# Gating tables of a product-key expert layer: GpSimd makes finished rows for two of four token groups, ScalarE scales the other two, VectorE none

## What is computed

```python
def peer(h, w_q, subkeys, u_tab, v_tab):     # 8 heads, 128 x 128 = 16384 experts, top 16
    q = (xb @ w_q).reshape(PEER_BLOCK, PEER_HEADS, PEER_QDIM)
    ...
    e = i1 * PEER_N_KEYS + i2                # 8 x 16 experts per token
    g = softmax(cs)                          # and a gate for each
    a = gelu(einsum('pd,phkd->phk', xb, u_tab[e]))
    return einsum('phk,phkd->pd', g * a, v_tab[e])
```

## Time and profile before

| | |
|---|---|
| median of 3 executions | 3304.9 us (3303.24 to 3307.88) |
| the profiled execution, its time | 3311.35 us |
| the profiled execution, its span in the trace | 3309.6 us |
| busy PE, DVE, ACT, POOL | 93%, 51%, 50%, 46% of the span |
| gating stage of layer 0 | about 695 to 805 us |
| gating stage of layer 1 | about 1815 to 1925 us |

### The profile page before, as it was taken

The page is one execution under the profiler, slowest core; times in us unless marked ns, Lnnn a source line. Parts: engine busy times, 40 slices in busy tenths (PEclk is TensorE's granted clock), DMA queues, the critical chain, the costliest instruction groups (busy, mean ns, idle before and its releaser), DMA issues.

```text
span 3309.6 us, 56035 instructions
## 1 busy us (share of the span) xinstructions
PE 3078.3 (93%) x18286; PEld 2726.7 (82%) x18286; DVE 1702.8 (51%) x2944; ACT 1666.8 (50%) x3149; POOL 1528.7 (46%) x1220
## 2 busy tenths in 40 slices
PE   8989999987999987999899699999999989999998
PEld 7679999976778866889899677877678779999997
DVE  6633370047888835173400878886301425555555
ACT  2123777788455533167677965555113224555554
POOL 3957998875444443178888644442551000000000
PEclk8979999999999997999999999999999979999999
DMA  6535554521766642345455056664664224555554
GB/s 246 195 133 181 171 171 165 182 78 57 254 228 226 231 141 89 132 140 179 157 179 176 0 184 241 234 222 139 210 208 142 91 81 154 187 186 184 184 185 132
DMA packets 153450, 552.42 MB, mean 167 GB/s; under 512 B 16896, under 2 KB 19712, under 8 KB 153232
## 3 DMA queue, kind: packets, MB, share of 16 engines
q1 hardware_dynamic: 151136, 547.42, 48.7%
q10 hardware_dynamic: 2224, 3.87, 0.4%
HBM read 550.17 MB, written 1.05 MB: 167 GB/s over the span
## 4 chain that ended last, share of the span: by engine, by line
PE 69%; ACT 9%; issue 8%; POOL 7%; DVE 4%; DMA 2%; ACTq 0%; DVEq 0%; POOLq 0%; SPq 0%; PEldq 0%
PE bank L901 19%; PE bank L875 16%; PE bank L1164 11%; PE bank L668 10%; PE bank L1182 5%; ACT hT L1352 5%; POOL w_parts L2285 4%; ACT hT L1348 2%; POOL arena L2317 1%; POOL arena L2319 1%; PE bank L687 1%; DMA ring<-stream 1%; PE bank L1146 1%; DMA arena<-stream 1%; PE bank L630 1%
## 5 line engine op out<-in xcount | busy, mean ns | idle before, releaser
L2285 POOL TENSOR_TENSOR w_parts<-ring,w_parts 128x512 fp32r<-128x512 f32 x512 | 687.2, 1368 | 193.6 <-ACT w_parts L1312 188.8
L875 PE MATMUL bank<-h_parts,w_parts 128*128 128x256 f32 x6144 | 747.5, 284 | 25.1 <-POOL w_parts L2285 23.1
L875 PEld LDWEIGHTS bank<-h_parts,w_parts 128*128 128x128 f32 x6144 | 743.2, 193 | 29.8 <-POOL w_parts L2285 26.8
L1312 ACT ACTIVATE w_parts<-ring 128x512 fp32r<-128x512 f32 x512 | 321.6, 630 | 205.6 <-PE bank L875 201.6
L668 PE MATMUL bank<-hT,ring 128*128 128x256 f32 x1584 | 361.8, 391 | 40.2 <-ACT hT L1245 32.4
L2236 DVE TENSOR_TENSOR w_parts<-ring,w_parts 128x512 fp32r<-128x512 f32 x384 | 265.3, 692 | 244.8 <-ACT w_parts L1505 236.9
L668 PEld LDWEIGHTS bank<-hT,ring 128*128 128x128 f32 x1584 | 308.4, 196 | 92.7 <-issue 33.6
L1164 PEld LDWEIGHTS bank<-h_parts,w_parts 128*128 128x128 f32 x3072 | 374.9, 193 | 5.6 <-issue 3.3
L1164 PE MATMUL bank<-h_parts,w_parts 128*128 128x256 f32 x3072 | 375.8, 284 | 2.6 <-DVE w_parts L2236 2.6
L1505 ACT ACTIVATE w_parts<-ring 128x512 fp32r<-128x512 f32 x384 | 242.2, 632 | 267.7 <-PE bank L1164 174.7
L901 PE MATMUL bank<-h_parts,a_parts 128*128 128x512 f32 x1536 | 366.2, 394 | 6.1 <-DVE a_parts L1995 6.1
(11 more groups left out here) (317 smaller groups left out, 4086.2 us busy)
## 6 DMA issues: line engine op xcount, KB each, us to landing
ring<-stream SPq DMA_DIRECT2D x786, 512.0 KB, 3.3
arena<-stream SPq DMA_DIRECT2D x192, 512.0 KB, 4.3
hT<-stream SPq DMA_DIRECT2D x32, 512.0 KB, 4.4
mean<-stream SPq DMA_DIRECT2D x32, 512.0 KB, 4.5
arena<-consts ACTq DMA_DIRECT2D x1, 1536.0 KB, 6.8
xT<-xin ACTq DMA_DIRECT2D x1, 1024.0 KB, 10.6
out<-hT SPq DMA_DIRECT2D x4, 256.0 KB, 2.2
arena<-subk ACTq DMA_DIRECT2D x2, 128.0 KB, 2.1
```

What stands on the lines that cost most here:

```text
L875: mm = pe.matmul(bank[k][:, 0:T], w[:, wp, ws], h_parts[:, hp, 4 * j + q, :], start=(j == 0 and q == 0 and i == 0), stop=(j == 1 and q == ...
L1312: act.activation(w_parts[half % HALVES][:, 0, :], ring[slot_][:, j * 512:(j + 1) * 512], ACT.Copy).then_inc(sem(f"{n}_high"), 1)
L2285: pool.tensor_tensor(w[:, 1, :], ring[(base + k) % RING][:, j * 512:(j + 1) * 512], w[:, 0, :].bitcast(F32), ALU.subtract).then_inc(sem(f" ...
```

## The change

Group 3 moves from ACT and group 1 from DVE, both to POOL. For these two groups POOL no longer subtracts but makes the finished rows, token by token, with one instruction for each of the four tokens: (row of 0..127 == index) * gate, index and gate being columns of `route`. So POOL issues two instructions of 128x512 and eight of 128x128 in a turn, where it issued four of 128x512. ACT keeps the groups 0 and 2. DVE's `picked` and its copy of the gates go. POOL's loop over the turns is written out. The semaphores follow: `diff` counts two groups a turn, and `made_hot` takes the place of `picked_hot`.

```diff
-SCALED_G = (0, 2, 3)
-PICKED_G = 1
+SCALED_G = (0, 2)
+MADE_G = (1, 3)
...
-                    if k == PICKED_G:
-                        pe.wait_ge(sem(f"{n}_picked_hot"), it + 1)
+                    if k in MADE_G:
+                        pe.wait_ge(sem(f"{n}_made_hot"), it * len(MADE_G) + (MADE_G.index(k) + 1))
...
-                    act.wait_ge(sem(f"{n}_diff"), it * GROUPS + (k + 1))
+                    act.wait_ge(sem(f"{n}_diff"), it * len(SCALED_G) + (i + 1))
...
-            iota_p, gates_p = bank[0][:, 0:P], bank[0][:, P:P + T]
-            dve.tensor_copy(iota_p, iota)
-            dve.tensor_copy(gates_p, route[:, 2, :]).then_inc(signal("dve_step"), 1)
+            iota_p = bank[0][:, 0:P]
+            dve.tensor_copy(iota_p, iota).then_inc(signal("dve_step"), 1)
...
-            def picked(it):
-
-                k = PICKED_G
-                dve.wait_ge(sem(f"{n}_diff"), it * GROUPS + (k + 1))
-                part = hot1[:, 4 * k:4 * k + 4, :]
-                dve.scalar_tensor_tensor(part, part, 0.0, gates_p[:, bass.ds(it * TURN + 4 * k, 4)].unsqueeze(2)
-                                         .broadcast_to([P, 4, P]), ALU.is_equal, ALU.mult).then_inc(sem(f"{n}_picked_hot"), 1)
...
-            with pool.Fori(0, T // TURN) as it:
+            for it in range(T // TURN):
                 for k in range(GROUPS):
+                    tokens = slice(it * TURN + 4 * k, it * TURN + 4 * k + 4)
 
                     pool.wait_ge(sem(f"{n}_hot_free"), it * GROUPS + (k + 1))
-                    pool.tensor_tensor(hot1[:, 4 * k:4 * k + 4, :], iota.unsqueeze(1).broadcast_to([P, 4, P]),
-                                       route[:, 0, bass.ds(it * TURN + 4 * k, 4)].unsqueeze(2).broadcast_to([P, 4, P]),
-                                       ALU.subtract).then_inc(sem(f"{n}_diff"), 1)
+                    if k in SCALED_G:
+                        pool.tensor_tensor(hot1[:, 4 * k:4 * k + 4, :], iota.unsqueeze(1).broadcast_to([P, 4, P]),
+                                           route[:, 0, tokens].unsqueeze(2).broadcast_to([P, 4, P]),
+                                           ALU.subtract).then_inc(sem(f"{n}_diff"), 1)
+                    else:
+                        for s, t in enumerate(range(tokens.start, tokens.stop)):
+                            ins = pool.tensor_scalar(hot1[:, 4 * k + s, :], iota, route[:, 0, t:t + 1],
+                                                     route[:, 2, t:t + 1], ALU.is_equal, ALU.mult)
+                        ins.then_inc(sem(f"{n}_made_hot"), 1)
```

More of the change, by code:

```diff
@@ L1962, in ones2 @@
                                   ALU.is_equal).then_inc(sem(f"{n}_hot2"), 1)
-            def picked(it):
-                k = PICKED_G
-                dve.wait_ge(sem(f"{n}_diff"), it * GROUPS + (k + 1))
-                part = hot1[:, 4 * k:4 * k + 4, :]
-                dve.scalar_tensor_tensor(part, part, 0.0, gates_p[:, bass.ds(it * TURN + 4 * k, 4)].unsqueeze(2)
-                                         .broadcast_to([P, 4, P]), ALU.is_equal, ALU.mult).then_inc(sem(f"{n}_picked_hot"), 1)
             for k in range(GROUPS):
                 ones2(0, k)
-                if k == PICKED_G + 1:
-                    picked(0)
             with dve.Fori(0, T // TURN - 1) as it:
@@ L1979, in peer_dve @@
                     ones2(it + 1, k)
-                    if k == PICKED_G + 1:
-                        picked(it + 1)
             for k in range(GROUPS):
```

## The result

The changed kernel takes **3354.4 us** in the median (3350.7 to 3361.9), the kernel before 3306.4 in the same comparison: ratio **1.0144**, 95% interval 1.0118 to 1.0170. I had forecast 3261.4 us in a range of 3243 to 3308. The change made the kernel 48 us slower, and it went the way of rival (d), further than its bounds reached.

What follows compares the result with a forecast made beforehand. ACT's three groups, 6.6 us a turn, were taken to bound the gating stages. POOL's turn of 2.0 + 8p would replace them, saving 145.2 - 248p, 43.5 us at p = 0.41: 3261.4 us, range 3243 to 3308.

Steps and rivals of the forecast that it cites:

- rival (d): Gating stages: POOL's queue replaces ACT's and is slower, from p = 0.585; 3317 us at p = 0.635; chance 0.14.
- What bounds the kernel: Gating stages: a turn costs three ACT groups of 2.20 us, 6.6 us; the stage is 109.9 us per layer.
- The terms for ACT, DVE and PE: Per gating turn: ACT loses 2.20 of 6.6 us, leaving 4.4; DVE falls to 4.8; PE stays at 4.1 to 4.6.
- DVE's limit of 4.8 us: Gating turn: four table products and four comparisons left on DVE, 8 x 0.60 us, the floor if POOL is cheaper.
- POOL's price p: Start-to-start time of POOL's new 128x128 instruction in the gating stages, taken as 0.41 us from the 128x128 addition.
- 145.2 - 248p: Microseconds saved over both layers' gating stages, p in us; 43.5 at 0.41, nothing left at 0.585.
- The bounds of p: POOL's new instruction: low end 0.355 us from subtraction's element cost, high end 0.706 us, the dearest 128x128 row.
- The figures of the Trainium skill: POOL's new instruction: 1.03 cycles an element gives p = 0.25; two reads of 102 cycles, 0.17 us, would make 0.58.
- What costs nothing: Gating stages: POOL's written-out loop of 160 instructions a layer, ACT's short instructions and the `hot_free` waits were given zero.
- `hot_free` waits: Before POOL's groups: already met, as group 2 is free after some 3.7 us and POOL returns after 4.3.
- The tail of 5.3 us: End of the gating stage, after group 2's subtraction: ACT 2.3, PE 1.16 and 0.9, DVE 0.69, hand-overs 0.25 us.
- The range: Whole kernel: 3243 to 3308 us, from DVE's floor up through no difference; the slower case, chance 0.14, left out.

Runs made afterwards that it cites:

- e9: Changed kernel with POOL's groups 1 and 3 made by one 128x512 mult, mult and two 128x256 instructions, gates and rows left out; 3249.6 us once.
- e3: Kernel before with only POOL's loop over the turns written out; ratio 0.9992 (0.9983 to 1.0002).
- e1: Changed kernel with POOL's eight 128x128 instructions of a turn in eight different forms, to price them; 3308.1 us once.
- e2: Changed kernel with one POOL instruction of 128x512 in place of each four of 128x128; 3280.6 us once.
- e10: Changed kernel with other operations in POOL's eight 128x128 instructions of a turn, gates and rows left out; 3319.0 us once.
- e5: Changed kernel with mult in place of is_equal in POOL's eight instructions of a turn, comparison left out; ratio to the kernel before 0.9870.
- e6: Kernel before with only group 1 moved from DVE to POOL, group 3 staying with ACT, POOL's loop written out; ratio 1.0020.

## Why the prediction was wrong, point by point

*What bounds the kernel: right.* ACT's three groups set the turn. Where they were made two, some other queue set it in every run, and always the longest by the sums.

*The terms for ACT, DVE and PE: right.* DVE's limit of 4.8 us was met in e9. In the kernel after, ACT's two groups of 2.2 us and its two waits of 1.79 us make 8.0 us of POOL's turn of 8.2.

*POOL's price p: wrong, and with it the forecast.* This is the step that failed: "I take p = 0.41 us". Measured 0.772. The rule of the sum, 145.2 - 248p, gives with it 46.3 us lost against 46.9 in the two stages and 48.0 in the medians. So the mechanism and the sum were right, and one term was nearly twice as large as I had it. Its parts, by the runs: I had 0.186 fixed, 128 x 1.67 ns = 0.214 for the elements and 0.055 for scalars and second operation, less 0.045 of overlap. The instruction has 128 x 3.34 = 0.427 for the elements, 0.15 for the two scalars and 0.22 fixed, less 0.02 of overlap. Of the 0.427, 0.11 is the second operation, so scalars and second operation come to 0.26 where I had left 0.055.

*The bounds of p: wrong too.* I bounded a form of instruction that the trace didn't hold from above by 0.706 us, the dearest row of its size, an addition in another stage that shares neither its operations nor its operands. It wasn't even the dearest execution: 0.706 is that row's median, and the same rows go up to 714 and 1318 ns. That the elements themselves could cost more than in any row was not in the range, though two rows of one engine, at 2.1 and 1.67 ns, already differed by the form. Rival (d) had the right sign and the right place, and two scalars as its reason; of the 0.36 us between 0.41 and 0.772 the elements are 0.21, and scalars and the larger fixed part together the rest.

*The figures of the Trainium skill.* In the prediction stood the Trainium skill, GPSIMD Engine Reference, section 3.1, with 1.03 cycles an element for one input and at most two operations. The runs show 0.83 ns an element for the pair mult, mult only. For is_equal, mult they show 3.34 ns, and at 128 elements four other pairs cost the same. By an estimate with the 1.2 GHz of that page of the Trainium skill, the first is near 1 cycle and the second 4. Section 7 of that page of the Trainium skill has 102 cycles for a small read command, by an estimate 85 ns; a scalar from SBUF cost 69 to 81 ns. The same section of the Trainium skill names 4 cycles an element for a chain of dependent operations. That is the number measured, but mult, mult is two operations in a row as well and doesn't cost it, and no run here shows the reason.

*What costs nothing: right* for the written-out loop (e3) and for the `hot_free` waits, as POOL doesn't wait for PE between 700 and 830 us. The tail of 5.3 us was right too: in layer 0 it took 5.2 us from the end of group 2's subtraction to the end of the last table product. The down stages moved whole, but for 4.3 us in one of them.

*The range* left out just the side on which the result lay. It gave 0.14 to slower; for a price bounded only by rows of other forms that was too little.

## What to carry to other kernels

When work moves to an engine in a form of instruction that the trace doesn't hold, the form is to be priced first, at two lengths, in the place where it will run; one run with eight forms at eight lines did it here. A steep sum (2.5 us for every 10 ns) on an unmeasured term deserves a range as wide as the term's, not as the neighbours'. And move no more than until the next queue is as long: with two of the eight tokens of a turn moved (and two left with ACT, four with DVE) the kernel gained 1.1%, with ACT's four 0.66%, with DVE's four it lost 0.2% and with all eight 1.4%.

## What the runs showed of the hardware

GpSimd's tensor_scalar on 32-bit floats costs 3.34 ns an element for the pair (is_equal, mult), at 64 to 512 elements (after, e1, e2, e9). The pairs (is_ge, mult), (max, mult), (subtract, mult) and (mult, is_equal) cost the same as it at 128 elements, 797 to 809 ns (e10). Only (mult, mult) costs 0.83 ns an element (e9). One operation is no way out: a comparison alone costs about 2.5 ns an element, by an estimate from e1 and e2, and a single mult takes 614 ns at 128 elements where the pair takes 451 (e10). Each scalar that comes from SBUF costs 69 to 81 ns more than a constant in its place (e1, e10). What is left is a fixed part of about 0.2 us.

In e5, with eight short forms a turn, the durations grew while the steps did not: the subtractions showed 1098 ns in the median against 1040 elsewhere, and the (mult, mult) instruction 509 against 444 in e1, while the steps stayed at 1.03 and 0.42 us. A duration on this engine is no step, and the steps are what adds up.

The granted clock of the stages was 0.95 before and 0.84 after, but it doesn't simply follow PE's idle time: between 697 and 780 us PE is busy 62% in e1 and in the kernel after, at 0.98 and 0.84. What a stretch at a low clock costs depends on the slack behind it. The kernel before lost nothing to two stretches at 0.76, and e6, with POOL 0.5 us a turn below ACT, lost 1.2 to 1.5 us to each of three such stretches.
